# Layer 0's paired projection products: four plain blocks and fourteen couples, the whole activation rows copied by ScalarE, and a new order of splits and windows

## The reference, cut to what matters

```python
def pool_mixer(h, w_in, w_group, scale, w_out):        # layer 0
    proj = h @ w_in                                    # 1024x1024 @ 1024x4096
    u, gate = proj[..., :POOL_WIDTH], proj[..., POOL_WIDTH:]
    ug = u.reshape(B, S, len(POOL_WINDOWS), POOL_GROUP)          # windows 2, 4, 8, 16
    pooled = jnp.stack([centred_window_mean(ug[:, :, g], w) for g, w in enumerate(POOL_WINDOWS)], axis=2)
    diff = pooled - ug
    mixed = jnp.einsum('bsgc,gcd->bsgd', diff, w_group).reshape(B, S, POOL_WIDTH) * scale
    return (mixed * jax.nn.silu(gate)) @ w_out

def reference(...):                                    # two layers
    x = x + pool_mixer(rms_norm(x, ...), ...)          # layer 0
    x = x + dilated_attention_mixer(rms_norm(x, ...), ...)       # layer 1, not touched by the change
```

## Time and profile before

| | us |
|---|---|
| median of 3 runs (lowest, highest) | 1845.68 (1844.07, 1845.81) |
| the profiled execution's own time | 1844.97 |
| its span, first to last instruction | 1842.4 |
| TensorE busy | 1797.6 (98%) |
| VectorE busy | 991.0 (54%) |
| ScalarE busy | 594.6 (32%) |
| GpSimd busy | 264.3 (14%) |

### The profile page before, as it was taken

How to read it: one execution, slowest core, us unless ns; L and a number is a source line. 1 busy time by engine, 2 the same in 40 slices (tenths; PEclk the granted TensorE clock), 3 DMA queues, 4 the chain that set the end, 5 groups by cost and what they waited for, 6 DMA issues and landing times.

```text
span 1842.4 us, 23147 instructions
## 1 busy us (share of the span) xinstructions
PE 1797.6 (98%) x8820; PEld 1512.2 (82%) x8820; DVE 991.0 (54%) x1824; ACT 594.6 (32%) x1092; POOL 264.3 (14%) x296
## 2 busy tenths in 40 slices
PE   7979999999999999999999999999999999999999
PEld 6868777788888788888889888888888888888887
DVE  6776767664665743454156425523585415532575
ACT  4333333322121422343245424323421323422420
POOL 3242433100000411111011201110100101110100
PEclk9999999999999999999999999999999999999999
DMA  5123222472422421111111111111245111111234
GB/s 173 59 103 129 100 92 92 160 297 91 137 69 81 141 71 48 45 58 59 46 41 53 47 46 46 58 46 35 70 162 181 47 46 41 52 46 46 70 115 160
DMA packets 100876, 159.31 MB, mean 86 GB/s; under 512 B 15520, under 2 KB 53280, under 8 KB 100768
## 3 DMA queue, kind: packets, MB, share of 16 engines
q1 hardware_dynamic: 82368, 115.26, 19.8%
q10 hardware_dynamic: 18400, 42.58, 6.4%
HBM read 120.01 MB, written 37.81 MB: 86 GB/s over the span
## 4 chain that ended last, share of the span: by engine, by line
PE 87%; DVE 8%; POOL 2%; DMA 1%; issue 1%; ACT 1%; ACTq 0%; SPq 0%; DVEq 0%; POOLq 0%
PE pair L807 25%; PE pair L809 25%; PE pair L808 25%; PE pair L1088 4%; PE pair L1066 4%; PE pair L1056 2%; PE pair L1075 2%; DVE bufU L1262 2%; DVE bufS L1262 1%; DVE w L1141 1%; DMA raw<-in_pool_w_in_dram 1%; DVE bufS L1174 1%; DVE ubuf L1267 1%; POOL side L777 0%; PE pair L820 0%
## 5 line engine op out<-in xcount | busy, mean ns | idle before, releaser
L807 PE MATMUL pair<-w,hTh 128*128 128x512 f32 x1280 | 515.3, 403 | 0.8 <-DVE xs L1150 0.8
L809 PE MATMUL pair<-w,hTl 128*128 128x512 f32 x1280 | 500.7, 391 | 0.0
L808 PE MATMUL pair<-w,hTh 128*128 128x512 f32 x1280 | 499.4, 390 | 0.0
L809 PEld LDWEIGHTS pair<-w,hTl 128*128 128x128 f32 x1280 | 244.2, 191 | 50.6
L807 PEld LDWEIGHTS pair<-w,hTh 128*128 128x128 f32 x1280 | 244.6, 191 | 45.2 <-DVE xs L1150 1.0
L808 PEld LDWEIGHTS pair<-w,hTh 128*128 128x128 f32 x1280 | 245.0, 191 | 43.9
L1135 DVE TENSOR_TENSOR w<-raw,w 128x1024 fp32r<-128x1024 f32 x113 | 137.1, 1223 | 251.9 <-ACT w L1590 251.1
L1877 ACT ACTIVATE pp<-pp,stat 128x256 f32<-128x256 f32 (+1 forms) x192 | 89.4, 466 | 240.4 <-DVE stat L1448 240.4
L797 POOL TENSOR_SCALAR qvar<-qss 128x4 f32<-128x4 f32 x96 | 25.1, 261 | 959.2 <-DVE qss L1417 959.2
L1417 DVE TENSOR_REDUCE qss<-qn 128x4 f32<-128x512 f32 x96 | 65.8, 686 | 158.3 <-ACT qn L1842 157.6
L1590 ACT ACTIVATE w<-raw 128x1024 fp32r<-128x1024 f32 x117 | 122.3, 1053 | 48.4 <-DMA raw<-in_pool_w_group_dram 21.9
(11 more groups left out here) (184 smaller groups left out, 2891.0 us busy)
## 6 DMA issues: line engine op xcount, KB each, us to landing
raw<-in_att_w_in_dram SPq DMA_DIRECT2D x80, 512.0 KB, 3.7
raw<-in_pool_w_in_dram SPq DMA_DIRECT2D x32, 512.0 KB, 5.0
diff_spill<-ubuf SPq DMA_DIRECT2D x16, 512.0 KB, 2.6
raw<-in_pool_w_out_dram SPq DMA_DIRECT2D x16, 512.0 KB, 4.5
stage<-gate_spill SPq DMA_DIRECT2D x16, 512.0 KB, 5.0
u_spill<-ub ACTq DMA_DIRECT2D x32, 256.0 KB, 2.3
ub<-u_spill SPq DMA_DIRECT2D x32, 256.0 KB, 3.7
xb<-x_spill ACTq DMA_DIRECT2D x16, 512.0 KB, 4.5
```

Of the source, the lines that this page charges most:

```text
L807: nc.tensor.matmul(out, lh, rh, start=first, stop=False, skip_group_check=onto)
L808: nc.tensor.matmul(out, lh, rl, start=False, stop=False, skip_group_check=onto)
L809: return nc.tensor.matmul(out, ll, rh, start=False, stop=last, skip_group_check=onto)
```

## The change

- `PLAIN` is four U blocks; the two plain G blocks become part of G couples, of which there are now eight: 14 couples, in turn G and U, beginning with G, with two G at the end.
- The ring of split weights has eight granules (`w0x` is gone); the room of `w0x` holds the weight sums (`sums`, a tensor of its own). `weight_sums(0)` no longer waits for the plain G blocks.
- `put_together` is gone. ScalarE copies each transposed block a second time, whole (`keep_whole`), for blocks 2 to 7, and VectorE takes it from there for the low part; blocks 0 and 1 are put together by one VectorE operation. TensorE's transposes wait for `whole_set` where they waited for `hlo_done`.
- `turned_sums`, `turned_high`, `turned_low` and the splits of couple 0 are in another order, and two halves of `tone` change places.
- The window means of a U couple's second block are done in two parts around `add_quarter(n, 1)` of the couple behind it; the first block's stay at the end of their couple.
- ScalarE's copies (`keep`) and splits are in another order; SyncE loads two small constants that ScalarE's queue loaded.
- `row_lead`, 128 bytes per partition, moves layer 1's buffers behind it by as much.

```diff
-    PLAIN = [("U", 0, 0), ("U", 0, 1), ("U", 0, 2), ("U", 0, 3), ("G", 0, 0), ("G", 0, 1)]
+    PLAIN = [("U", 0, c) for c in range(GB)]
     u_couples = [("U", g, h) for g in range(1, NG) for h in range(GB // 2)]
-    g_couples = [("G", 0, 1)] + [("G", g, h) for g in range(1, NG) for h in range(GB // 2)]
-    COUPLES = [k for both in zip(u_couples, g_couples) for k in both] + g_couples[len(u_couples):]
+    g_couples = [("G", g, h) for g in range(NG) for h in range(GB // 2)]
+    COUPLES = [k for both in zip(g_couples, u_couples) for k in both] + g_couples[len(u_couples):]
     NCOUPLE, NPROD = len(COUPLES), 7
 
...
-    R0, R1, RAW, GRANULES = 4, 6, 2, 10
+    R0, R1, RAW, GRANULES = 4, 6, 2, 8
...
-        return u % (GRANULES // 2) if u < NPLAIN else (u - LATER + 2) % R0
+        return u % R0 if u < NPLAIN else (u - LATER + 1) % R0
 
     def granule(n, i):
 
-        return (2 * (NPLAIN % (GRANULES // 2)) + NPROD * n + i) % GRANULES
+        return (NPROD * n + i) % GRANULES
...
             with ExitStack() as spare:
-                w0x = sb("w0x", [P, 1, 2, 1024], F32R, spare)
+                sums = sb("sums", [P, 4, 512], F32, spare)
...
-                if u == NPLAIN + 1:
+                if u == 3:
+                    load_constants()
+                if u == NPLAIN + 3:
...
                         store_diff(0, c)
-                elif NPLAIN + 1 < u < LATER and u % 2:
-                    n = (u - NPLAIN) // 2 - 1
...
+                elif NPLAIN + 3 < u < LATER and u % 2:
+                    kind, g, h = COUPLES[(u - NPLAIN) // 2 - 2]
+                    if kind == "U":
+                        store_diff(g, 2 * h)
+                        store_diff(g, 2 * h + 1)
...
-                    inverse_roots(layer, *range(5))
-                    for tb in range(TB):
-                        put_together(tb)
-                        if tb < 3:
-                            inverse_roots(layer, 5 + tb)
+                    inverse_roots(layer, *range(TB))
...
                     pool.wait_ge(w_lo, product(n - 1, 5) + 1)
-                else:
-                    pool.wait_ge(g_done, 2)
                 a11, a12, a21, a22 = (raw[:, 0, 0:512], raw[:, 0, 512:1024], raw[:, 1, 0:512], raw[:, 1, 512:1024])
-                nc.gpsimd.tensor_tensor(sums[0], a21, a22, ALU.add).then_inc(s_sum, 1)
+                nc.gpsimd.tensor_tensor(sums[:, 0, :], a21, a22, ALU.add).then_inc(s_sum, 1)
...
-                if tb and n > 1:
+                if layer == 0 and n > 2:
+                    pe.wait_ge(whole_set, n - 2)
+                elif tb and n > 1:
...
             for job in PLAIN[3:]:
...
+                pe.wait_ge(whole_set, TB - 2)
...
                         pe.wait_ge(kept, 3 * n + 1)
                         if n == 0:
+                            pe.wait_ge(t_lo, 3)
+                    elif i == 3:
+                        if n == 0:
                             pe.wait_ge(t_lo, 4)
...
-                                            x_pair(layer, tb)[:, :].rearrange("p (k c) -> p k c", k=KD),
+                    src = x_pair(layer, tb)[:, :].rearrange("p (k c) -> p k c", k=KD)
+                    if layer == 0 and tb >= 2:
+                        dve.wait_ge(whole_set, tb - 1)
+                        src = whole[:, :, P * tb:P * tb + P]
+                    nc.vector.tensor_tensor(rowsl[:, :, P * tb:P * tb + P], src,
                                             rowsh[:, :, P * tb:P * tb + P].bitcast(F32), ALU.subtract).then_inc(hlo_done, 1)
...
                 def scale(tb):
...
-                        split_lo(tb // 2 + 1)
+                        if tb < 6:
+                            split_lo(tb // 2 + 1)
                         lows(tb + 1)
+                        if tb == 2:
+                            first = slice(0, 2 * P)
+                            dve.wait_ge(hlo_done, 2)
+                            dve.wait_ge(hlo_half, 1)
+                            link(nc.vector.tensor_tensor(whole[:, :, first], rowsh[:, :, first].bitcast(F32),
...
-                dve.wait_ge(whole_set, TB)
+                dve.wait_ge(whole_set, TB - 2)
+                dve.wait_ge(dve_step, steps[0])
                 nc.vector.tensor_tensor(b22, b22, b12, ALU.subtract).then_inc(t_sum, 1)
...
-            def window(g, c):
+            def window(g, c, part=None):
 
                 w, q = WINDOWS[g], c % 2
+                if part != 1 and GB * g + c:
+                    dve.wait_ge(d_ready, GB * g + c)
                 u = ubuf[:, q, :]
...
+                    if part is None or part == n // 2:
+                        link(nc.vector.tensor_tensor(dst[:, lo:lo + num], src[:, lo + a:lo + a + num],
+                                                     src[:, lo + b:lo + b + num], ALU.add))
+                    src, spare_, k, n = dst, spare_[::-1], 2 * k, n + 1
+                if part == 0:
+                    return
...
-            def couple_windows(n):
+            def first_window(n):
 
                 kind, g, hh = COUPLES[n]
...
+                kind, g, hh = COUPLES[n]
+                if kind == "U":
                     dve.wait_ge(c21_done, n + 1)
-                    window(g, 2 * hh + 1)
+                    window(g, 2 * hh + 1, part)
...
-            split_lo(5)
-            for i in range(4):
-                turned_low(i)
+            turned_low(0)
+            turned_low(1)
+            split_product(0, 0)
+            split_product(0, 1)
+            turned_low(2)
+            for i in range(2, NPROD):
+                split_product(0, i)
+            turned_low(3)
             dve.wait_ge(xt_done, TB)
+            dve.wait_ge(const_in, 16 * 2)
             plain_window(0)
             plain_window(1)
-            split_product(0, 0)
-            split_product(0, 1)
-            plain_window(2)
-            plain_window(3)
-            for i in range(2, NPROD):
-                split_product(0, i)
...
             split_product(1, 0)
             split_product(1, 1)
-            add_quarter(0, 1)
-            split_product(1, 2)
             add_quarter(0, 2)
-            for i in range(3, NPROD):
+            plain_window(2)
+            for i in range(2, NPROD):
                 split_product(1, i)
-            couple_windows(0)
-            for i in range(3):
-                split_product(2, i)
+            plain_window(3)
             for n in range(1, NCOUPLE):
+                add_quarter(n, 0)
                 if n < NCOUPLE - 1:
-                    split_product(n + 1, 3)
-                    add_quarter(n, 0)
-                    for i in range(4, NPROD):
+                    for i in range(5):
                         split_product(n + 1, i)
+                    second_window(n - 1, 0)
                     add_quarter(n, 1)
+                    second_window(n - 1, 1)
+                    split_product(n + 1, 5)
                     add_quarter(n, 2)
-                    couple_windows(n)
-                    if n < NCOUPLE - 2:
-                        for i in range(3):
-                            split_product(n + 2, i)
-                    else:
-                        split_lo(LATER)
+                    split_product(n + 1, 6)
+                    first_window(n)
                 else:
-                    add_quarter(n, 0)
-                    split_lo(LATER + 1)
+                    split_lo(LATER)
                     diff_low(0, 0)
                     diff_low(0, 1)
                     add_quarter(n, 1)
                     diff_low(0, 2)
                     diff_low(0, 3)
+                    split_lo(LATER + 1)
...
                 p = NPROD * n + i
-                if p >= GRANULES - 2:
-                    act.wait_ge(*((prod_done, p - GRANULES + 1) if p >= GRANULES else (g_done, 2)))
-                elif p < 6:
...
+                if p < GRANULES:
+                    act.wait_ge(u_done, p // 2 + 1)
                 else:
-                    act.wait_ge(g_done, 1)
+                    act.wait_ge(prod_done, p - GRANULES + 1)
...
+                    act.wait_ge(xt_done, tb + 1)
+                    nc.scalar.activation(whole[:, :, P * tb:P * tb + P],
+                                         x_pair(0, tb)[:, :].rearrange("p (k c) -> p k c", k=KD),
+                                         ACT.Copy).then_inc(whole_set, 1)
...
                         highs(tb)
-                        split_hi(tb // 2 + 1)
+                        keep_whole(tb)
+                        if tb < 6:
+                            split_hi(tb // 2 + 1)
                         highs(tb + 1)
+                        keep_whole(tb + 1)
...
             copy_u(0)
-            split_hi(5)
             copy_u(1)
-            for i in range(4):
-                turned_high(i)
-            plain_gate(0)
+            turned_high(0)
             split_product(0, 0)
             split_product(0, 1)
+            turned_high(1)
+            turned_high(2)
```

(33 more changed lines are left out.)

96 lines of the change are left out of this document (34 added, 62 removed).

## The result

The changed kernel takes **1831.4 us** (median of 4 runs, 1830.46 to 1833.45) against 1844.88 for the kernel before beside it: ratio 0.9929, 95% interval 0.9911 to 0.9946. It is faster by 13.5 us, where 24.7 were forecast; the time lies 0.4 us above the range's end. The profiled execution's span is 1828.7 us against 1842.4.

What follows compares the result with a forecast made beforehand. TensorE, busy 98% of the span, was taken as the bound, so matmul count and its waits decide. −2.7 − 1.9 − 12.9 − 7.2 = −24.7 from 1844.97 gave 1820.3, stated as 1820.5 us, range 1814 to 1831.

Steps and rivals of the forecast that it cites:

- Term 1: Matmuls: two plain G blocks (96) go, a 14th couple (84) comes, −2.7 us.
- Term 2: Layer 0's start: waits fall from 4.27 to 2.3 us with put_together gone from GpSimd, −1.9 us.
- Term 3: Waits in the couples: 11.3 for 24.2 us, −12.9; 6.3 in six G couples, 4.4 in couple 1.
- The walk: Engine operations summed from a couple's start S: addition done S + 17.3, product 6 due S + 16.32.
- signs of being wrong: A wait of 4 us or more left, couples' pitch above 20.1 us everywhere, or layer 1's 317 us changed.
- signs of being right: Couples from about 70 to 348 us, 11 us of waits, clock 1.00 from 60 to 348, scaling 1.28.
- The rest. Couple 0 and couples 3 to 13: 0.6 by the same walk.: Couples other than couple 1 and the six G couples behind U couples: 0.6 us of waits in all.
- The rival "slower": Late raw loads stop TensorE at product 4 in every couple, 13 x 3.3 = 43, 1863 us; chance 0.03.
- No wait of mine passes 2.7, so the 7.2 us go.: Clock in the couples: slower matmuls behind long waits vanish, −7.2 us (bound −3.6).
- Terms 3 and 4: Waits in the couples, −12.9 us, and slower matmuls from clock drops there, −7.2 us.
- The rival "the waits are longer": Couple 1's late loads and clock drop +9, slower window passes in six couples +6; 1826.5 to 1835.5 us; chance 0.16.
- The forecast's rival by that rule: Start: GpSimd/VectorE port as exclusive lock, a low part waits out a 1.99 us addition; 1822.3 us; chance 0.01.

Runs made afterwards that it cites:

- the run in one piece: The changed kernel with the second block's window whole ahead of add_quarter 1, as before, all else kept: 1843.09 us, ratio 0.9985.
- the first experiment: The changed kernel with the second block's window moved whole between splits 1 and 2 in VectorE's list: 1830.55 us, ratio 0.9915.

## Why the prediction was wrong

**Right.** What bounds the kernel, and the mechanisms of terms 1 and 2, and of term 3 for the G couples and couple 1. Term 1: 12 matmuls fewer. Term 2: waits of the start 2.3 (0.75, 0.57, 0.49 and 0.49, for 1.1 and three of 0.4), the scaling 1.28 (but 2.29 in the last block, beside a weight sum), the couples' beginning 0.6 us early. Its −1.9 is against the kernel before. Within the new order GpSimd's work, left in, costs 7.7 us, since the turned sums are then late and four plain blocks do not cover them, the condition that the term names. Term 3, the G couples: 0.82 to 0.85 of idle time, 0.98 from start to start, for 1.05; the run in one piece gives the same walk's other values to 0.1 us. Couple 1: the raw load at 95.32 was worked out as 95.3, and the loss is the 4.4 us forecast. It came as waits of 2.08 and 0.17 and 1.8 of slower matmuls, for waits of 2.7 and 1.7. The slower matmuls cost nothing here: where the clock did not fall behind the first wait, the second one was 1.81, and product 6 started just as late (7.5 us after the first wait's end in both). TensorE with the second window earlier, in order of time:

```profile
102.90 0.50 PE L804 MATMUL pair<-ttwo,w 128*128 128x512 f32 x1 [2.08 <-ACT side L1720]
...
110.44 0.50 PE L804 MATMUL pair<-ttwo,w 128*128 128x512 f32 x1 [1.81 <-DVE ubuf L1298]
```

Of the forecast's signs of being wrong none appeared (the longest wait is 3.56 us). What did not appear either are two of its signs of being right: 11 us of waits, and a clock of 1.00 throughout.

**Wrong, first: "The rest. Couple 0 and couples 3 to 13: 0.6 by the same walk."** It was 8.2 us of waits. The walk went by the chain's load of 5.04 us, 5.6 to 5.8 from issue to the first sum in the kernel before. In U couples it is now 8 to 9, because the change lets these loads start at the moment when the gate's stores start: the loads come behind the second window in VectorE's list, the gates behind the couple's end in ScalarE's. Moving the stores alone removed these waits. The walk also had the splits at 0.60 each; beside GpSimd's late sums three took 3.38 instead of 1.90. The rival "slower" named just this price (a load's time under company, up to 11.9 us) and the place (behind the two splits); what it did not see is that a late load reaches TensorE through `add_quarter(n, 1)` behind the splits of sums well before it does at product 4. The last couple's 3.56 us, the largest single wait, was missed outright: its addition stands behind low parts of `diff`, whose loads are issued at 338.9 and land at 351; the prediction has no term for them.

**Wrong, second: "No wait of mine passes 2.7, so the 7.2 us go."** Three waits brought the clock down again, 1.7 us of slow matmuls each, 5.1 in all. The one in couple 1, at 2.08 us a forecast wait, cost nothing, as said; those in couple 11 and in the last couple, behind waits that the walk did not have, cost their 3.4. The term rested on a bound between 1.63 (none) and 4.2 us (one) that no row gave. Over all the runs, up to 360 us, slow matmuls came behind some waits from 1.79 us on and behind all from 3.56 on, and did not come behind others, the longest of 2.52, 2.84, 3.44 (one of two) and 3.48 us. Part of the old 7.2 was also no clock at all: counted from start to start the three slow stretches hold 4.9; the rest are the small losses behind every wait, and the modelled ends.

**The sum.** −2.7 and −1.9 stand. Terms 3 and 4 together gave 31.4 − 23.5 = 7.9 us instead of 20.1. The 12.2 missing are 5.4 in the last couple, 3.7 in couple 11, 2.2 in U couples 5, 7 and 9, 0.3 in the G couples and 0.6 not placed. Less 0.6 at the start and 0.5 behind the couples, they are the 11 us by which the profiled span missed.

**The rival "the waits are longer" (0.16)** was the nearer case: 1831.4 lies within its 1826.5 to 1835.5, and it named late loads and the clock; but it put them in couple 1 alone, where the loss was the forecast one, and its window passes beside GpSimd were not there: in the couples every pass took 1.22 to 1.24 us. That its number fits is in good part luck. The passes stand beside GpSimd only when they are moved earlier, as the first experiment did.

**Where the gain came from.** One split moved in ScalarE's list of the old kernel gives 9.4 us of the 13.5. The window in two parts is worth 12 us within the new order, because that order puts five splits ahead of the addition. So they aren't shares of one sum; how the parts would add from the old kernel was not tried step by step.

## What to carry to other kernels

A load's duration from a quiet place of the trace holds only there: where a change moves its issue, list what the other queues issue in the next few microseconds and take the load's time under that company. In engines with strict lists, walk each dependence through every operation that stands ahead, not only through the one that is waited for first; here a late load hurt through an addition that does not read it. And price a clock drop as possible, not as absent, for each wait of about 1.8 us or more; then ask whether something later in the same couple is late enough to hide it, as in couple 1.

## What the runs showed of the hardware

The clock: how long TensorE waited does not alone decide whether 1.2 GHz follows. Behind 3.44 us the clock was 1.00 once and fell once, in one execution. Couple 1's first wait was 2.0 to 2.2 us in seven profiled executions of six kernels. It ended at 101.2 to 101.8 us in five of them, and the clock fell behind it in all five; it ended at 102.9 and 103.0 in the other two, and the clock fell in neither. The Trainium skill (TensorE: Matmul & The Clock Gate, "Part 1: The HAM clock gate") says that the monitor runs free of the kernel, so the moment would count beside the length. The runs agree that the length alone does not decide; why the clock fell at the same place in five executions, if the monitor is free of the kernel, they leave open.

GpSimd and VectorE: in the changed kernel GpSimd's sum starts at 44.80 and takes 1.28 us, to 46.08, and VectorE's low part, from SBUF, shows 2.33 us from 44.84.

```profile
44.84 2.33 DVE L1168 TENSOR_TENSOR hTl<-whole,hTh 128x1024 fp32r<-128x1024 f32 x1 [1.14 <-ACT whole L1636]
```

```profile
44.80 1.28 POOL L775 TENSOR_TENSOR sums<-raw 128x512 f32<-128x512 f32 x1
46.03 2.29 POOL L777 TENSOR_TENSOR sums<-raw,sums 128x512 f32<-128x512 f32 x1
```

46.08 + 1.1 is 47.2, the low part's end, and 47.17 + 1.15 is 48.32, the next sum's. The last block's scaling, from 41.40, does the same behind the sum that ends at 42.61 (2.29 us, to 43.69). Each waits for the whole of the other, and the wait counts as busy time. That is the exclusive lock of the Trainium skill (SBUF — State Buffer, "two separate sides"). The forecast's rival by that rule was right in its mechanism, on the low part before the last, which cost 1.1 us more than alone (1.0 by the forecast's rows). Slack hid it: the last low part starts at 48.57 and takes 1.23 us, and the start's waits add up to the forecast 2.3.
